# Splitting each weight slot in four passes of 512 columns on GpSimd, and waiting for half a slot on TensorE

## The chip, the cores and the metric

The kernel runs on one core of a Trainium2 chip. The metric is the device time of one execution, in microseconds (us). One profiled execution is read for the prediction; a small number of others were timed without a profile.

## What is computed

Two layers of an encoder trunk over 512 tokens of width 1024, in float32. Each layer is, cut to what matters:

```
h = layer_norm(ALPHA*h + 0.5*swiglu(h, ffn1_wg, ffn1_wu, ffn1_wd))      # 1024 -> 2816 -> 1024
u = h @ w_in                                                            # 1024 -> 8480 columns
y_rw, y_sb, y_hg = rwkv7(u), stick_breaking_attention(u), hgrn2(u)      # three token mixers
mix = (g_rw*(y_rw@w_br_rw) + g_sb*(y_sb@w_br_sb) + g_hg*(y_hg@w_br_hg)) @ w_out
h = layer_norm(ALPHA*h + mix)
h = layer_norm(ALPHA*h + 0.5*swiglu(h, ffn2_wg, ffn2_wu, ffn2_wd))
h = layer_norm(ALPHA*h + sigmoid(h@ple_gate) * (p@ple_proj))
```

Nearly all of the arithmetic is in the dense products with weights that come from HBM.

## The kernel before, in words

**Products.** TensorE works in fp32r, a float32 of fewer mantissa bits. To keep float32 accuracy each operand is split into a high part and a rest: `hT` (the activations, `hT_hi` and `hT_lo`) and the weights (`w_hi` and `w_lo`). A product is three matmuls, high by high, rest by high and high by rest, added up in one PSUM bank (L838, in `products`).

**Slots.** The weights pass through in 468 slots, in a fixed order (`dense_groups`). A slot is 256 rows of a weight matrix, so two blocks `kk` of 128 rows, by up to 512 columns: 128 partitions by 2 by 512 elements. 428 slots have all 512 columns, 32 (the r, k, v projections) have 384, and 8 (the low-rank inputs) have 288. SyncE loads them into `w_raw`, a ring of three (`RAW_RING`). GpSimd splits slot `n` in two passes, each over both blocks at once: L1081 adds a zero and rounds, which gives `w_hi`; L1084 subtracts `w_hi` from the raw weight, which gives `w_lo`. Both go to rings of three slots (`SPLIT_RING`). Between the two passes GpSimd waits on a semaphore of its own (`w_high`), and before a slot it waits for the load and for the release of slot `n-3` by TensorE. SyncE refills a place of `w_raw` after L1084 of its slot.

**TensorE's loop.** `dense` waits for `w_rest_ready` of a slot, which L1084 sets, and then runs for `kk` 0 and 1 over the (mostly four) tiles `m`, three matmuls each: 24 matmuls of 512 columns for a full slot. The release of the slot is set on its last matmul. Where `own_x` is given, block `k` of the activations is waited for as well (`hT_rest`, set by VectorE at L1536; `yT_rest` at L1785; `act_rest`; `mT_rest`). In a group with a `tail`, the last slots are read by all `m` in turn, so that banks finish one after another.

**VectorE.** It has the splits of the activations (L1535 and L1536; L1582 and L1583; L1784 and L1785; L1812 and L1813), the layer norms (L1542 to L1551, then L1570 and L1571, which rescale the residual, eight instructions of 1024 elements), the merge of the branches (L1805 and L1809) and the arithmetic of the mixers (among it L1719 to L1728 of HGRN2, and L578 to L649 of RWKV-7). In the mixers TensorE's order is written by hand: blocks of dense products (`fill`) are put between the mixers' small matmuls.

## Time and profile before

| | us |
|---|---|
| median of 3 runs | 3225.05 |
| lowest and highest | 3222.54 and 3225.9 |
| the profiled execution | 3221.0 |
| its span, first to last instruction | 3219.2 |
| TensorE busy | 3045.5 |
| GpSimd busy | 2104.3 |
| VectorE busy | 1589.3 |

The profiled execution lies 4 us below the median. In the profile PE is TensorE's matmuls, DVE is VectorE, POOL is GpSimd, ACT is ScalarE, and L with a number is a line of the kernel. A duration of POOL or DVE runs from its start to its end, and so includes time in which the instruction was held up after it had started. The ends of matmuls are modelled and reach over the next one's start, so that their pace is read from the distance of the starts.

### The profile page before, as it was taken

The page shows a single profiled execution, that of the slowest core. Times are in us where ns is not written, and L with a number is a line of the kernel's source. Part 1 is how long each engine was busy: PE and PEld are TensorE (multiplying, and loading weights), DVE is VectorE, ACT ScalarE, POOL GpSimd, SP SyncE. Part 2 cuts the span into 40 slices and gives each one's busy share as a digit, 9 for nine tenths or more (in the row PEclk, how much of TensorE's full clock was granted, in tenths as well). Part 3 has the DMA queues.
Part 4 walks back from the last instruction along what each step waited for, and adds up shares of the span by engine and source line. Part 5 has one row for each costly group of instructions (what it writes and reads, how often), then busy time and mean ns, then how long its engine had stood idle before and what let it go on. Part 6 is the DMA issues. An engine that isn't in the chain of part 4 may idle for free. (4 is left out here: it accounts for less than half of the span.)

```text
span 3219.2 us, 45211 instructions
## 1 busy us (share of the span) xinstructions
PE 3045.5 (95%) x19506; PEld 2502.9 (78%) x19506; DVE 1589.3 (49%) x1811; ACT 566.0 (18%) x915; POOL 2104.3 (65%) x941
## 2 busy tenths in 40 slices
PE   8999999889999999999899999998899999999996
PEld 6888787777777878888688887777777778788875
DVE  5321334766656683221882215248666486722127
ACT  1000025443310010000110000353433100100000
POOL 7888675322238878887788877753221578788874
PEclk9999999999999999999899999999999999999998
DMA  4333332111113333323223323311210123333231
GB/s 139 98 96 96 98 118 60 42 49 31 31 40 97 119 97 104 97 94 98 92 92 98 98 93 104 105 55 35 55 40 22 60 88 122 104 99 93 97 105 66
DMA packets 202019, 267.75 MB, mean 83 GB/s; under 512 B 12352, under 2 KB 130460, under 8 KB 201692
## 3 DMA queue, kind: packets, MB, share of 16 engines
q1 hardware_dynamic: 195200, 244.82, 25.1%
q10 hardware_dynamic: 6620, 20.04, 1.8%
q8 instruction: 154, 2.52, 0.3%
q14 instruction: 45, 0.37, 0.0%
HBM read 258.52 MB, written 6.29 MB: 82 GB/s over the span
## 5 line engine op out<-in xcount | busy, mean ns | idle before, releaser
L1081 POOL TENSOR_TENSOR w_hi<-w_raw,zero 128x1024 fp32r<-128x1024 f32 (+2 forms) x468 | 945.7, 2021 | 1040.1 <-PE ps L838 1029.5
L1084 POOL TENSOR_TENSOR w_lo<-w_raw,w_hi 128x1024 fp32r<-128x1024 f32 (+2 forms) x468 | 1160.7, 2480 | 36.8
L838 PE MATMUL ps<-hT_hi,w_hi 128*128 128x512 f32 x2288 | 917.0, 401 | 18.2 <-DVE hT_lo L1536 10.1
L838 PE MATMUL ps<-hT_lo,w_hi 128*128 128x512 f32 x2288 | 897.0, 392 | 0.0
L838 PE MATMUL ps<-hT_hi,w_lo 128*128 128x512 f32 x2288 | 896.7, 392 | 0.0
L838 PEld LDWEIGHTS ps<-hT_hi,w_hi 128*128 128x128 f32 x2288 | 431.7, 189 | 118.5 <-issue 16.5
L838 PEld LDWEIGHTS ps<-hT_hi,w_lo 128*128 128x128 f32 x2288 | 431.8, 189 | 92.7
L838 PEld LDWEIGHTS ps<-hT_lo,w_hi 128*128 128x128 f32 x2288 | 432.5, 189 | 89.0 <-issue 2.9
L1579 DVE TENSOR_TENSOR act_raw<-silu,ps 128x512 f32<-128x512 f32 x88 | 59.8, 680 | 555.7 <-PE ps L838 555.7
L838 PE MATMUL ps<-w_hi,aT_hi 128*128 128x512 f32 x704 | 274.2, 390 | 0.0
L838 PE MATMUL ps<-w_lo,aT_hi 128*128 128x512 f32 x704 | 273.9, 389 | 0.0
L838 PE MATMUL ps<-w_hi,aT_lo 128*128 128x512 f32 x704 | 273.9, 389 | 0.0
L1599 DVE SCALAR_TENSOR_TENSOR h_tok<-ps,h_tok 128x512 f32<-128x512 f32 x48 | 32.7, 681 | 422.5 <-PE ps L838 422.5
L1195 ACT ACTIVATE silu<-ps 128x512 f32<-128x512 f32 x88 | 52.6, 598 | 903.1 <-PE ps L838 899.5
L838 PEld LDWEIGHTS ps<-w_hi,aT_hi 128*128 128x128 f32 x704 | 132.2, 188 | 27.4
L838 PEld LDWEIGHTS ps<-w_hi,aT_lo 128*128 128x128 f32 x704 | 132.2, 188 | 27.4
L838 PEld LDWEIGHTS ps<-w_lo,aT_hi 128*128 128x128 f32 x704 | 132.2, 188 | 27.4
L1583 DVE TENSOR_TENSOR aT_lo<-act_raw,aT_hi 128x512 fp32r<-128x512 f32 x88 | 144.1, 1637 | 3.0
L838 PE MATMUL ps<-w_hi,hT_hi 128*128 128x512 f32 x320 | 129.5, 405 | 4.7 <-DVE hT_lo L1536 4.7
L838 PE MATMUL ps<-w_lo,hT_hi 128*128 128x512 f32 x320 | 126.6, 395 | 0.0
L838 PE MATMUL ps<-w_hi,hT_lo 128*128 128x512 f32 x320 | 126.5, 395 | 0.0
L1582 DVE CAST aT_hi<-act_raw 128x512 fp32r<-128x512 f32 x88 | 109.6, 1246 | 3.0
(297 smaller groups left out, 3667.3 us busy)
## 6 DMA issues: line engine op xcount, KB each, us to landing
w_raw<-in_w_in SPq DMA_DIRECT2D x104, 512.0 KB, 3.6
w_raw<-in_ffn_wg SPq DMA_DIRECT2D x176, 256.0 KB, 2.8
w_raw<-in_ffn_wu SPq DMA_DIRECT2D x176, 256.0 KB, 3.1
w_raw<-in_ffn_wd SPq DMA_DIRECT2D x88, 512.0 KB, 3.6
w_raw<-in_w_in SPq DMA_DIRECT2D x96, 128.0 KB, 2.3
w_raw<-in_w_out SPq DMA_DIRECT2D x16, 512.0 KB, 3.7
w_raw<-in_ple_gate SPq DMA_DIRECT2D x16, 512.0 KB, 3.6
ln_rows<-in_ln_g ACTq DMA_DIRECT2D x8, 512.0 KB, 3.9
```

Source lines behind the costliest of these rows:

```text
L838: ins = nc.tensor.matmul(o, l_, r_, start=first, stop=last)
L1081: nc.gpsimd.tensor_tensor(w_split[0][:, q, :, 0:w], w_raw[:, r, :, 0:w], zero[:, 0:1].unsqueeze(2).to_broadcast([P, 2, w]), ALU.add).then_ ...
L1084: nc.gpsimd.tensor_tensor(w_split[1][:, q, :, 0:w], w_raw[:, r, :, 0:w], w_split[0][:, q, :, 0:w].bitcast(F32), ALU.subtract).then_inc(*st ...
L1195: nc.scalar.activation(silu[:, m, :], b[:, :], ACT.Silu).then_inc(*step("silu_done", L, f, g, m))
L1579: v.tensor_tensor(act_raw[:, m, :], silu[:, m, :], b[:, :], ALU.mult).then_inc(*step("act_raw", L, f, g, m))
L1582: chain(v.tensor_copy(aT[0][:, k, :], act_raw[:, m, :]))
L1583: v.tensor_tensor(aT[1][:, k, :], act_raw[:, m, :], aT[0][:, k, :].bitcast(F32), ALU.subtract).then_inc(*step("act_rest", L, f, k))
L1599: v.scalar_tensor_tensor(z, b[:, :], 0.5 if name == "down" else 1.0, z, ALU.mult, ALU.add).then_inc(*step("res_sum", L, q, half, m))
```

## The change

GpSimd splits a slot in four passes instead of two: for `kk` 0, high part and rest over its columns, then the same for `kk` 1. The semaphores count each half: `w_high` and `w_rest_ready` are set twice for a slot. The wait between high part and rest is kept in each half. TensorE waits for `w_rest_ready` of half `kk` ahead of that half's matmuls; in a tail it waits for the second half, which follows the first on GpSimd. SyncE waits for the second half. Rings, order, loads, the release of slots and all arithmetic are unchanged.

```diff
--- before.py
+++ after.py
@@ -847,8 +847,8 @@
                 at_slot[0] += len(slots)
                 head = len(slots) - tail
                 for i in range(head):
-                    pe.wait_ge(*after("w_rest_ready", n0 + i))
                     for kk in range(2):
+                        pe.wait_ge(*after("w_rest_ready", n0 + i, kk))
                         if own_x is not None:
                             own_x(2 * i + kk)
                         for m in range(n_tiles):
@@ -857,7 +857,7 @@
                 for m in range(n_tiles):
                     for i in range(head, len(slots)):
                         if m == 0:
-                            pe.wait_ge(*after("w_rest_ready", n0 + i))
+                            pe.wait_ge(*after("w_rest_ready", n0 + i, 1))
                         for kk in range(2):
                             if own_x is not None and m == 0:
                                 own_x(2 * i + kk)
@@ -1078,11 +1078,13 @@
                 pool.wait_ge(*after(f"w_in{r}", n))
                 if n >= SPLIT_RING:
                     pool.wait_ge(*after(*slot_free[n - SPLIT_RING]))
-                nc.gpsimd.tensor_tensor(w_split[0][:, q, :, 0:w], w_raw[:, r, :, 0:w],
-                                        zero[:, 0:1].unsqueeze(2).to_broadcast([P, 2, w]), ALU.add).then_inc(*step("w_high", n))
-                pool.wait_ge(*after("w_high", n))
-                nc.gpsimd.tensor_tensor(w_split[1][:, q, :, 0:w], w_raw[:, r, :, 0:w],
-                                        w_split[0][:, q, :, 0:w].bitcast(F32), ALU.subtract).then_inc(*step("w_rest_ready", n))
+                for kk in range(2):
+                    nc.gpsimd.tensor_tensor(w_split[0][:, q, kk, 0:w], w_raw[:, r, kk, 0:w], zero[:, 0:1].to_broadcast([P, w]),
+                                            ALU.add).then_inc(*step("w_high", n, kk))
+                    pool.wait_ge(*after("w_high", n, kk))
+                    nc.gpsimd.tensor_tensor(w_split[1][:, q, kk, 0:w], w_raw[:, r, kk, 0:w],
+                                            w_split[0][:, q, kk, 0:w].bitcast(F32), ALU.subtract).then_inc(
+                        *step("w_rest_ready", n, kk))
 
 
         @block.sync
@@ -1101,7 +1103,7 @@
                     pieces, g, i = slot_list[n]
                     r = n % RAW_RING
                     if n >= RAW_RING:
-                        sp.wait_ge(*after("w_rest_ready", n - RAW_RING))
+                        sp.wait_ge(*after("w_rest_ready", n - RAW_RING, 1))
                     if g[0][0] == "rkv" and g[0][2] == 1 and i == 3:
                         load_rwkv(g[0][1])
                     for src, at, w in pieces:
```

## Rows read from the trace of the kernel before

**Rows 1.** The page, part 1: engine, busy us, share of span, instructions.

```profile
PE 3045.5 (95%) x19506; PEld 2502.9 (78%) x19506; DVE 1589.3 (49%) x1811; ACT 566.0 (18%) x915; POOL 2104.3 (65%) x941
```

**Rows 2.** Waits of TensorE: waiter, awaited, us in total, times, longest.

```profile
PE ps L894 <- DVE h_tok L1551: 29.6, 15, 4.2
...
PE ps L838 <- DVE hT_lo L1536: 14.8, 7, 2.3
...
PE ps L838 <- POOL w_lo L1084: 4.0, 1, 4.0
```

**Rows 3.** Timeline of GpSimd: start us, duration us, what, idle time before.

```profile
55.13 1.89 POOL L1081 TENSOR_TENSOR w_hi<-w_raw,zero 128x1024 fp32r<-128x1024 f32 x1 [1.01 <-PE ps L838]
...
57.10 2.38 POOL L1084 TENSOR_TENSOR w_lo<-w_raw,w_hi 128x1024 fp32r<-128x1024 f32 x1
...
564.67 1.15 POOL L1081 TENSOR_TENSOR w_hi<-w_raw,zero 128x576 fp32r<-128x576 f32 x1 [1.00 <-PE ps L838]
...
565.89 1.40 POOL L1084 TENSOR_TENSOR w_lo<-w_raw,w_hi 128x576 fp32r<-128x576 f32 x1
```

**Rows 4.** Timeline of TensorE where one slot ends, another begins.

```profile
409.10 0.39 PE L838 MATMUL ps<-hT_hi,w_lo 128*128 128x512 f32 x1
...
409.33 0.39 PE L838 MATMUL ps<-hT_hi,w_hi 128*128 128x512 f32 x1
```

**Rows 5.** Windows: us, busy us of each engine, granted clock; last column GB/s.

```profile
109.53:131.29 21.76, 21.76 (x98) 18.02 (x97) 6.58 (x6) 1.20 (x2) 18.18 (x8) 1.00 0.32 97
...
16.00:20.00 4.00, 4.00 (x11) 3.13 (x11) 3.96 (x3) 0.00 (x0) 3.92 (x2) 0.57 0.41 131
```

**Rows 6.** Timeline of the start, three engines.

```profile
13.36 2.40 POOL L1084 TENSOR_TENSOR w_lo<-w_raw,w_hi 128x1024 fp32r<-128x1024 f32 x1
...
13.60 2.71 DVE L1536 TENSOR_TENSOR hT_lo<-h_raw,hT_hi 128x512 fp32r<-128x512 f32 x1
...
15.81 0.50 PE L838 MATMUL ps<-hT_hi,w_hi 128*128 128x512 f32 x1 [3.99 <-POOL w_lo L1084]
...
18.38 2.75 DVE L1536 TENSOR_TENSOR hT_lo<-h_raw,hT_hi 128x512 fp32r<-128x512 f32 x1
...
35.64 0.50 PE L838 MATMUL ps<-hT_hi,w_hi 128*128 128x512 f32 x1 [1.75 <-DVE hT_lo L1536]
```

**Rows 7.** Timeline, VectorE, without a GpSimd pass beside it.

```profile
36.57 0.42 DVE L1535 CAST hT_hi<-h_raw 128x512 fp32r<-128x512 f32 x1
...
37.02 0.69 DVE L1536 TENSOR_TENSOR hT_lo<-h_raw,hT_hi 128x512 fp32r<-128x512 f32 x1
```

**Rows 8.** Timelines after a norm, GpSimd's passes and TensorE's first use.

```profile
404.23 2.87 POOL L1081 TENSOR_TENSOR w_hi<-w_raw,zero 128x1024 fp32r<-128x1024 f32 x1
...
419.52 3.26 POOL L1084 TENSOR_TENSOR w_lo<-w_raw,w_hi 128x1024 fp32r<-128x1024 f32 x1
...
425.65 0.39 PE L838 MATMUL ps<-hT_hi,w_hi 128*128 128x512 f32 x1
```

**Rows 9.** Timelines of the first layer norm, VectorE and GpSimd.

```profile
384.89 2.48 DVE L1551 TENSOR_SCALAR h_tok<-h_tok,ln_mv,ln_rstd 128x1024 f32<-128x1024 f32 x1
...
384.94 1.89 POOL L1081 TENSOR_TENSOR w_hi<-w_raw,zero 128x1024 fp32r<-128x1024 f32 x1
```

**Rows 10.** Timelines of the merge, VectorE and TensorE.

```profile
1037.91 2.73 DVE L1785 TENSOR_TENSOR yT_lo<-y_raw,yT_hi 128x512 fp32r<-128x512 f32 x1
...
1035.94 0.47 PE L838 MATMUL ps<-yT_hi,w_hi 128*128 128x512 f32 x1 [0.76 <-issue]
...
1040.70 0.50 PE L838 MATMUL ps<-yT_hi,w_hi 128*128 128x512 f32 x1 [1.77 <-DVE yT_lo L1785]
```

**Rows 11.** Groups by line and shape: count, busy us, mean ns, idle us before.

```profile
L1721 DVE TENSOR_TENSOR hg_p<-hg_p 128x1024 f32<-128x1024 f32 x14 | 25.7, 1837 | 0.5
```

**Rows 12.** Timeline of VectorE in the HGRN2 part, one free instruction.

```profile
617.30 1.22 DVE L1721 TENSOR_TENSOR hg_p<-hg_p 128x1024 f32<-128x1024 f32 x1
```

**Rows 13.** Windows: the mixer of one layer.

```profile
560.00:935.00 375.00, 334.30 (x4524) 274.61 (x4523) 243.49 (x392) 140.20 (x222) 104.85 (x56) 0.96 0.13 36
```

## The prediction

> **What bounds the kernel now.** I read the page's busy line first, then the waits, then the timelines of single stretches. TensorE is busy for 95% of the span, GpSimd for 65% [rows 1]. So only some 174 us in which TensorE does nothing can be won, and the question is whom it waits for then. The waits say: mostly VectorE. Its layer norms hold TensorE for 29.6 us and the split of the activations for 14.8 us; GpSimd's split of the weights holds it once, for 4.0 us, at the start [rows 2]. That the change lets TensorE begin on half a slot is therefore worth little in itself. What can matter is that GpSimd and VectorE hold each other up, and that the change alters the size of the pieces.
>
> **How close GpSimd is to being the bound.** Where nothing disturbs it, a full slot costs GpSimd 1.89 us for the high part and 2.38 us for the rest [rows 3], 4.36 us with the gaps. TensorE starts a matmul every 0.227 us, with no gap where one slot ends and the next begins although a wait stands there [rows 4], so it takes 24 x 0.227 = 5.44 us for a slot. GpSimd has 1.08 us to spare for each slot. In a stretch of four slots of the first FFN layer with VectorE at work beside it, it was busy for 18.18 of 21.76 us [rows 5].
>
> **Part 1: the added passes.** A pass of half the size costs more than half. The passes over 1024 and 576 elements took 1.89 and 1.15 us (high part), 2.38 and 1.40 us (rest) [rows 3]: 1.65 and 2.19 ns for an element, so 0.20 and 0.14 us that don't shrink. A pass over 512 elements then takes 1.04 and 1.26 us. A slot becomes 2 x (1.04 + 1.26) + 2 x 0.08 (the wait between high part and rest) = 4.76 us, 0.40 us more than now; for the line's other end, a fixed part of nothing, it is 0.08 us more. Beside TensorE's 5.44 us both are hidden: in the FFN stretch 18.18 us of passes, 0.32 us of gaps and 4 x 0.40 give 20.1 of 21.76 us [rows 5]. Value taken: 0.40 us a slot on GpSimd, nothing on the path. If the cover is gone, each further 0.1 us on each of the 176 slots of the FFN's first products costs 18 us.
>
> **Part 2: the added waits.** TensorE gets a second wait in each slot. Queued behind it are that half's 12 matmuls. The half has long been ready, and a satisfied wait at a slot's boundary showed no gap [rows 4]: nothing. SyncE's wait, with the refill queued behind it, ends 0.40 us later, and that place of the three-deep ring is read only after two more slots: nothing. GpSimd's added wait is in the 4.76 us.
>
> **Part 3: the start.** TensorE's first product begins at 15.81 us, when the first slot is whole [rows 6]. With half a slot it begins 1.89 + 2.38 - 1.04 - 1.26 = 1.97 us earlier, at 13.84. Then TensorE needs a new block of activations every 12 x 0.227 = 2.72 us, but VectorE gives one only every 4.78 us (13.60 to 18.38 [rows 6]). Its two instructions need 0.42 and 0.69 us when alone [rows 7]; they are held up by GpSimd's passes: the one issued at 13.60 ends 0.55 us after the w_lo pass of 13.36 [rows 6]. So the pace is one pair of passes and 0.5 us. With half passes it is 1.04 + 1.26 + 0.5 and some 0.05 more, 2.85 us, and since TensorE starts with a block in hand, it no longer waits noticeably. The sixth block begins at 35.64 us now [rows 6]. It would begin at 13.84 + 5 x 2.72 + 1.5 = 28.9, where 1.5 us is what the half clock costs: in 4 us at a granted clock of 0.57 [rows 5] 11 matmuls ran in place of 17.6. Gain 6.7 us. Bounds: 2.0 us (the half slot alone, VectorE's pace unchanged) and 8.2 us (the shorter pause also spares the low clock).
>
> **Part 4: the merge.** At the end of the first half of the merge TensorE waits 0.76 and 1.77 us for the split of the next branch [rows 10]. VectorE has been busy without a break before that; one such instruction took 2.73 us in place of 0.69 [rows 7, 10]. In this stretch four tiles follow one another with three instructions each that a pass can hold up. Held up by half passes, each loses at most 1.0 to 1.3 us in place of 1.5 to 2.0, though more of them are hit; I take 0.5 us of gain for each of the last three tiles and 1 us for each block of the split, 3.5 us, which is more than the 2.5 us of waiting. Gain 2.5 us in each layer, 5.0 in all; bounds 0 and 5.0.
>
> **Part 5: the layer norms.** There are seven with TensorE waiting. In the first, VectorE's L1551 was issued at 384.89 us, waited through the pass of 384.94 to 386.83 and ended 0.54 us after it [rows 9]; alone it would need about 0.8 us. With half passes I laid the same instructions out. L1551 of the tile before is held up too, so this one is issued near 385.35, during a rest pass that ends near 385.7. If VectorE is let in then, it ends near 386.2 and TensorE's next product starts 0.9 us earlier than now. If GpSimd's queued high part goes first, as here, L1551 ends near 387.2, and the two instructions of the split behind it meet one pass each where one of them met none: 0.4 us later than now. Value: nothing; bounds over seven norms -6 and +3 us.
>
> The Trainium skill ("SBUF — State Buffer", Who interferes with whom) says that VectorE and GpSimd share one port pair, that an instruction holds it for its whole length, and that issue order decides who is blocked. This row speaks against the last of these: VectorE was issued 0.05 us ahead of the pass and still came after it. By the page's rule the norms would gain the 6 us; rival B is that case.
>
> **Part 6: the mixers.** Here VectorE often sets the end, and TensorE is idle for 41 of 375 us in a layer [rows 13]. The 14 instructions of L1721 took 1.84 us on the mean [rows 11] against 1.22 us when free [rows 12]: 0.6 us lost by each. An instruction that comes alone loses less to a half pass. In a dense chain, where each of VectorE's instructions meets a pass, what is lost is the whole time of the passes, and that grows from 4.27 to 4.60 us a slot. With some 25 slots in each layer's mixers, a third of that growth on VectorE and half of it on the path, this is 50 x 0.33 / 6 = 2.8 us lost; lone instructions give back 0.8. Value: +2 us; bounds -9 (0.6 us on some 45 instructions are 27 us of delay in a layer; halved, and a third of it felt, that is 4.5) and +20 us (0.4 us on each of 50 slots, all of it felt).
>
> **Part 7: the stretches where GpSimd falls behind.** After a norm L1570 and L1571, eight long instructions, alternate with the passes: the passes take 2.87 and 3.26 us, and a slot 6.2 us, more than TensorE's 5.44. The slot done at 422.78 us is first used at 425.65: 2.87 us ahead [rows 8]. Four such slots cost 3.0 us of the lead, which was 5.9. With four passes in a slot each meets one such instruction, which adds (2.87 - 1.89 + 3.26 - 2.38) / 2 = 0.93 us: a slot takes 4.76 + 3.7 = 8.5 us, but only two slots instead of four, since the eight instructions are used up sooner. That costs 6.1 us of the lead. But the pass that ends last is needed only 2.72 us after the slot's first product: 5.9 - 6.1 + 2.7 = 2.5 us stay. Nothing; if that cover is gone, 1 to 2 us in each of six places.
>
> **The sum.** -6.7 - 5.0 + 0 + 2.0 = -9.7 us. It is made against the profiled execution (span 3219.2 us, time 3221.0). The median of the runs lies 4 us above that, and I set the change against the median: 3225.05 - 9.7 = 3215.3 us.
>
> **The rivals.**
> A, forecast, 3215 us (its own range 3209 to 3221), chance 0.46.
> B, VectorE is let in at each end of a pass, so that none of its instructions loses more than one short pass: norms -6, mixers -9. 3225 - 6.7 - 5 - 6 - 9 = 3198 us. For it: at the start VectorE does come in after both kinds of pass [rows 6]. Against: the norm [rows 9]. Chance 0.17.
> C, only the start gains and the mixers take it back: -6.7 + 5 = 3223 us, no difference that can be measured. For it: one of the merge's two waits is put down to no one [rows 10], so the split needn't be what is late, and the bounds of parts 3, 4 and 6 allow it. Against: the two gains are on the path, TensorE stands still there [rows 6, 10]. Chance 0.21.
> D, slower: the dense chains. More passes stand in VectorE's way in the mixers, each taking its turn. Price up to 0.6 us a slot on 50 slots, 30 us, against 11.7 us gained: 3243 us. It decides from (11.7 + 6.5) / 50 = 0.36 us a slot. For it: VectorE is the late one there [rows 11, 12]. Against: the ports' added time is only 0.33 us a slot. Chance 0.11.
> E, slower too: GpSimd becomes the bound. If a pass has 0.15 us more of fixed time than the line gives, an FFN slot is 0.2 us over 5.44: 176 x 0.2 = 35 us, 3248 us. Chance 0.05.
>
> 0.2% (6.5 us) is about what a measurement of this kernel can tell from no change. Faster by more: B and five sixths of A (below 3218.6), 0.55. Within: C and the rest of A, 0.29. Slower: D, E, 0.16. The range leaves out D and E, 0.16, and takes in B and the slow side of C: 3196 to 3233 us.
>
> **What would show it.** TensorE's first product near 13.8 us and the sixth block near 29; passes of 1.04 and 1.26 us; the waits at the merge gone; L1551 in the norms still held up, by less; GpSimd near 20 of 21.76 us in an FFN stretch with TensorE's pace still 0.227 us; no wait of TensorE for w_lo after the start. A pass above 1.2 or 1.4 us, or VectorE's mixer instructions longer on the mean than now, would prove it wrong.

## The result, and the profile after

The changed kernel takes 3192.1 us (median of 4 runs, 3191.0 to 3193.9) against 3225.0 us for the kernel before on the same chip: a ratio of 0.990 (95% interval 0.988 to 0.992). It is 33 us faster, not 10, and lies 4 us below the range. The profiled execution took 3191.0 us with a span of 3189.2 us, so the traces differ by 30.0 us, and that is the amount that has to be found. Line numbers from L1081 on differ by one or two: L1081 and L1084 are now L1082 and L1085, L1535 and L1536 are L1537 and L1538, L1551 is L1553, L1721 is L1723, L1785 is L1787.

The page's busy line after:

```profile
PE 3035.5 (95%) x19506; PEld 2497.7 (78%) x19506; DVE 1401.0 (44%) x1811; ACT 566.3 (18%) x915; POOL 2316.1 (73%) x1877
```

Against [rows 1], TensorE runs the same 19506 matmuls in 10.0 us less busy time: summed over its trace the granted clock was at its lower level (1.2 GHz) for 129.8 us, before for 156.7. The other 20.0 us are pauses. VectorE, with the same 1811 instructions, is busy for 188 us less, and nothing of its own work was changed. GpSimd has twice the passes and 212 us more. So VectorE's instructions had been held up, and are held up less.

The waits of TensorE after (waiter, awaited, us in total, times, longest):

```profile
PE ps L894 <- DVE h_tok L1553: 23.8, 16, 3.8
PE ps L838 <- DVE hT_lo L1538: 19.0, 7, 3.2
...
PE ps L838 <- POOL w_lo L1085: 3.5, 2, 1.8
...
PE ps L539 <- DVE rhs L738: 1.7, 8, 0.2
...
PE ps L479 <- DVE invT L723: 1.1, 2, 0.6
```

Against [rows 2] the norms gave up 5.8 us and the split of the activations took 4.2 of them back. L539, RWKV-7's small matmuls inside the mixer, had 6.6 us in 14 waits before, the longest 1.4, and L479 had 5.0 us. Those two, which my prediction never looked at, gave back 8.8 us; L371 took 2.8 back (9.3 us in 6 waits, before 6.5 in 5).

By stage, from the starts of TensorE's matmuls at the stages' borders in the two traces, the 30.0 us are: the start 5.5; the mixers 7.9 and 5.8 (layer 0 and 1); the merge 3.7 and 5.2; the product with the embeddings and its norm (between the layers) 2.4; one FFN with its norm 1.1; some 1.5 us are lost again in small pieces. Each of these figures is the difference of one execution and one other. In parts of the mixers where nothing was changed such a difference reached 7.0 us (table at the last experiment), so the split by stages is rough, and what it says of single layers rougher still.

GpSimd's passes where nothing disturbs them (timeline of GpSimd: start us, duration us, what):

```profile
70.71 1.04 POOL L1082 TENSOR_TENSOR w_hi<-w_raw,zero 128x512 fp32r<-128x512 f32 x1
71.83 1.29 POOL L1085 TENSOR_TENSOR w_lo<-w_raw,w_hi 128x512 fp32r<-128x512 f32 x1
73.07 1.04 POOL L1082 TENSOR_TENSOR w_hi<-w_raw,zero 128x512 fp32r<-128x512 f32 x1
74.19 1.28 POOL L1085 TENSOR_TENSOR w_lo<-w_raw,w_hi 128x512 fp32r<-128x512 f32 x1
75.43 1.04 POOL L1082 TENSOR_TENSOR w_hi<-w_raw,zero 128x512 fp32r<-128x512 f32 x1
```

A slot takes 75.43 - 70.71 = 4.72 us there; 4.76 was worked out. Windows of the start and of an FFN stretch as in [rows 5] (same columns):

```profile
16.00:20.00 4.00, 4.00 (x18) 2.89 (x17) 3.96 (x4) 0.00 (x0) 3.92 (x4) 1.00 0.41 131
102.00:123.76 21.76, 21.76 (x98) 18.02 (x97) 6.02 (x6) 1.20 (x3) 20.86 (x18) 1.00 0.37 115
```

GpSimd is busy for 20.86 of 21.76 us in the second, where 18.18 stood before, and TensorE's pace is the same. In the first the granted clock is 1.00 where it was 0.57: 18 matmuls in 4 us, not 11.

The start, as in [rows 6], over all engines:

```profile
12.49 1.63 DVE L1538 TENSOR_TENSOR hT_lo<-h_raw,hT_hi 128x512 fp32r<-128x512 f32 x1
...
13.63 0.50 PE L838 MATMUL ps<-hT_hi,w_hi 128*128 128x512 f32 x1 [1.79 <-POOL w_lo L1085]
...
15.34 1.67 DVE L1538 TENSOR_TENSOR hT_lo<-h_raw,hT_hi 128x512 fp32r<-128x512 f32 x1
...
31.32 3.13 DVE L1643 TENSOR_SCALAR h_tok<-h_tok 128x4096 f32<-128x4096 f32 x1
...
32.37 3.19 POOL L1085 TENSOR_TENSOR w_lo<-w_raw,w_hi 128x512 fp32r<-128x512 f32 x1
...
35.62 0.50 PE L838 MATMUL ps<-hT_hi,w_hi 128*128 128x512 f32 x1 [1.70 <-POOL w_lo L1085]
```

The first product begins at 13.63 us and VectorE gives a block every 2.85 us, as worked out. The sixth block begins at 28.02 us, before at 35.64. Two things were missed. Beside VectorE's splits a pair of passes takes as long as VectorE's pair, a slot 5.76 us (passes at 13.54 and 19.30), more than TensorE's 5.44, so that GpSimd's lead shrinks. And then comes one long instruction of VectorE, L1643 over 4096 elements: the pass that starts at 32.37 takes 3.19 us instead of 1.29, and TensorE waits 1.70 us for its `w_lo` at 35.62. Before, the same instruction (L1641) came later, at 37.63.

**Where the mixers' gain sits.** RWKV-7 hands small results from TensorE to VectorE (L738) and back (L539), with one block of dense matmuls between. VectorE puts one long instruction of its own between two L738. Before (all engines, timeline):

```profile
812.54 2.14 DVE L626 TENSOR_TENSOR rw_dec<-k_inv,rw_e 128x512 f32<-128x512 f32 x1
...
814.74 2.71 DVE L630 SCALAR_TENSOR_TENSOR rw_kk<-rw_kk,rw_ss 128x512 f32<-128x512 f32 x1
...
814.87 0.27 PE L539 MATMUL ps<-rhs,pq 64*64 64x64 f32 x2 [0.23 <-DVE rhs L738]
...
817.37 0.21 DVE L738 TENSOR_TENSOR rhs<-ps,rhs 128x64 f32<-128x64 f32 x1
...
817.64 0.27 PE L539 MATMUL ps<-rhs,pq 64*64 64x64 f32 x2 [1.44 <-DVE rhs L738]
```

And after, the same instructions:

```profile
800.89 1.28 DVE L626 TENSOR_TENSOR rw_dec<-k_inv,rw_e 128x512 f32<-128x512 f32 x1
...
802.23 1.64 DVE L630 SCALAR_TENSOR_TENSOR rw_kk<-rw_kk,rw_ss 128x512 f32<-128x512 f32 x1
...
803.79 0.21 DVE L738 TENSOR_TENSOR rhs<-ps,rhs 128x64 f32<-128x64 f32 x1
...
804.18 0.27 PE L539 MATMUL ps<-rhs,pq 64*64 64x64 f32 x2
```

L630 is held up in both. An exchange with its dense block takes TensorE some 1.27 us (L539 at 812.02, next at 813.30). Before, L626 takes 2.14 us instead of 0.68 and TensorE stands still for 0.23 us; then L630 takes 2.71 instead of 0.68, and it stands still for 1.44 us. After, they take 1.28 and 1.64 us, and the dense work covers both: the row of L539 shows no idle time of TensorE ahead of it. So in this row of exchanges hold-ups of up to 1 us cost nothing, one of 1.5 us costs 0.2, and one of 2 us right behind it 1.4.

### The profile page after: what moved, and what is told of

Its sections match the earlier page's. It is cut to its first block and busy times, and to the rows that moved or that the text cites. A ratio compares the mean times of both kernels' runs of the same rounds, so it can differ in the third digit from the quotient of the medians.

```text
span 3189.2 us, 46255 instructions
## 1 busy us (share of the span) xinstructions
PE 3035.5 (95%) x19506; PEld 2497.7 (78%) x19506; DVE 1401.0 (44%) x1811; ACT 566.3 (18%) x915; POOL 2316.1 (73%) x1877
## 5 line engine op out<-in xcount | busy, mean ns | idle before, releaser
L1082 POOL TENSOR_TENSOR w_hi<-w_raw,zero 128x512 fp32r<-128x512 f32 (+2 forms) x936 | 1058.8, 1131 | 764.7 <-PE ps L838 754.6
L1085 POOL TENSOR_TENSOR w_lo<-w_raw,w_hi 128x512 fp32r<-128x512 f32 (+2 forms) x936 | 1283.3, 1371 | 73.5
L838 PE MATMUL ps<-hT_hi,w_hi 128*128 128x512 f32 x2288 | 916.0, 400 | 18.7 <-DVE hT_lo L1538 12.6
L838 PE MATMUL ps<-hT_hi,w_lo 128*128 128x512 f32 x2288 | 895.6, 391 | 0.0
L838 PE MATMUL ps<-hT_lo,w_hi 128*128 128x512 f32 x2288 | 895.6, 391 | 0.0
L838 PEld LDWEIGHTS ps<-hT_hi,w_hi 128*128 128x128 f32 x2288 | 431.0, 188 | 119.0 <-POOL w_lo L1085 15.6
L838 PEld LDWEIGHTS ps<-hT_hi,w_lo 128*128 128x128 f32 x2288 | 430.9, 188 | 92.9
L838 PEld LDWEIGHTS ps<-hT_lo,w_hi 128*128 128x128 f32 x2288 | 431.6, 189 | 88.2 <-issue 2.9
L838 PE MATMUL ps<-w_hi,aT_hi 128*128 128x512 f32 x704 | 274.3, 390 | 0.0
L838 PE MATMUL ps<-w_lo,aT_hi 128*128 128x512 f32 x704 | 274.0, 389 | 0.0
L838 PE MATMUL ps<-w_hi,aT_lo 128*128 128x512 f32 x704 | 273.9, 389 | 0.0
L838 PEld LDWEIGHTS ps<-w_hi,aT_lo 128*128 128x128 f32 x704 | 132.2, 188 | 27.5
L838 PEld LDWEIGHTS ps<-w_hi,aT_hi 128*128 128x128 f32 x704 | 132.2, 188 | 27.4
L838 PEld LDWEIGHTS ps<-w_lo,aT_hi 128*128 128x128 f32 x704 | 132.2, 188 | 27.2
L838 PE MATMUL ps<-w_hi,hT_hi 128*128 128x512 f32 x320 | 129.2, 404 | 6.4 <-DVE hT_lo L1538 6.4
L1585 DVE TENSOR_TENSOR aT_lo<-act_raw,aT_hi 128x512 fp32r<-128x512 f32 x88 | 126.6, 1439 | 3.0
L838 PE MATMUL ps<-w_hi,hT_lo 128*128 128x512 f32 x320 | 126.5, 395 | 0.0
L838 PE MATMUL ps<-w_lo,hT_hi 128*128 128x512 f32 x320 | 126.4, 395 | 0.0
L1179 ACT ACTIVATE ln_rstd<-ln_mv,ln_eps 128x1 f32<-128x1 f32 x32 | 9.4, 295 | 498.7 <-DVE ln_mv L1550 498.7
```

Source lines behind the costliest of these rows:

```text
L838: ins = nc.tensor.matmul(o, l_, r_, start=first, stop=last)
L1082: nc.gpsimd.tensor_tensor(w_split[0][:, q, kk, 0:w], w_raw[:, r, kk, 0:w], zero[:, 0:1].to_broadcast([P, w]), ALU.add).then_inc(*step("w_h ...
L1085: nc.gpsimd.tensor_tensor(w_split[1][:, q, kk, 0:w], w_raw[:, r, kk, 0:w], w_split[0][:, q, kk, 0:w].bitcast(F32), ALU.subtract).then_inc( ...
L1179: nc.scalar.activation(ln_rstd[:, t, :], ln_mv[:, t, 1:2], ACT.Sqrt, bias=ln_eps[:, :]).then_inc(*step("ln_sqrt", L, q, t))
L1585: v.tensor_tensor(aT[1][:, k, :], act_raw[:, m, :], aT[0][:, k, :].bitcast(F32), ALU.subtract).then_inc(*step("act_rest", L, f, k))
```

## The experiments

Two theories stood at the beginning. **H**: the time comes from VectorE being held up by shorter passes. **W**: it comes from TensorE's waits on half a slot. All kernels below have the following frame in place of the changed kernel's loop, with `split_parts` giving the passes of a slot as (first block, block after the last, first column, column after the last). Frame and changed kernel do the same where `split_parts` gives `[(0, 1, 0, w), (1, 2, 0, w)]`, a high and a rest pass over each half, four passes in all. The lines added at the top shift all numbers: L838 of before is L849 to L853 here, L1084 is L1097 to L1103. The kernel before was timed again beside each group of kernels, with medians from 3221.1 to 3224.4 us; where two kernels of different groups are compared, I give the difference of their gains too where it is another.

```diff
+        def last_part(n, kk):
+            return max(j for j, p in enumerate(parts_of(n)) if p[0] <= kk < p[1])
...
-                        pe.wait_ge(*after("w_rest_ready", n0 + i, kk))
+                        pe.wait_ge(*after("w_rest_ready", n0 + i, last_part(n0 + i, kk)))
...
-                for kk in range(2):
+                for j, (k0, k1, c0, c1) in enumerate(parts_of(n)):
```

### TensorE waits for the whole slot

```diff
 def split_parts(name, n, w):
     return [(0, 1, 0, w), (1, 2, 0, w)]
...
+                    pe.wait_ge(*after("w_rest_ready", n0 + i, last_part(n0 + i, 1)))
                     for kk in range(2):
-                        pe.wait_ge(*after("w_rest_ready", n0 + i, kk))
```

> Four passes for each slot as in the changed kernel, but TensorE waits for the whole slot at its top, as before the change. Theory H (short passes hold VectorE up for less): nearly all of the 33 us stay, and only the start loses 1 to 3 us, so 3193 to 3196 us. Rival W (what pays is that TensorE may begin on half a slot): most of the gain goes, 3215 us or more.

Measured: 3204.6 us, ratio 0.994 (0.992 to 0.996). Both theories missed; it lies between them. Its wait of TensorE for GpSimd:

```profile
PE ps L849 <- POOL w_lo L1099: 10.7, 10, 4.4
```

These are 10.7 us in ten waits, 7.2 more than after. By stages the mixers gain 7.1 and 4.7 us and the merge 3.7 and 5.2, where the changed kernel gains 7.9 and 5.8, 3.7 and 5.2: there the waits are worth little. Most of the 13.9 us between the two traces is lost at the start (3.0 us), in the first FFN of layer 1 (3.2), in the embeddings' stage (1.9) and at the end (2.2), places where GpSimd has fallen behind. So of the 33 us 18 to 20 need only the shorter passes, and 13 to 15 us need the half waits, as long as the FFNs have four passes (12.5 us between the medians of the two kernels, 13.9 between the traces, 15 between the gains).

### Four passes in the mixers and the merge alone

```diff
 def split_parts(name, n, w):
+    return [(0, 1, 0, w), (1, 2, 0, w)] if name[0] in ("sb", "hg", "lora", "rkv", "gate", "branch", "out") else [(0, 2, 0, w)]
```

> Four passes only for the slots of the mixers, the merge and the output projection (sb, hg, lora, rkv, gate, branch, out); two passes for all others. Between the two traces the mixers and the merge had shed 21.5 us of the 30. Theory H: 3225 - 21 = 3204 us, within 3 us. If the places interact (a shorter hold-up in one stage is given back in another) it is 3209 us or more.

Measured: 3193.4 us, ratio 0.991 (0.989 to 0.992), as fast as the whole change, and better than I expected. By stages: mixers 6.7 and 7.7 us, merge 3.7 and 5.2, the output product with its norm 1.4 in each layer, where the changed kernel loses 0.5. The FFNs' four passes and the start's gain come out even.

### Four passes everywhere else

```diff
 def split_parts(name, n, w):
+    return [(0, 2, 0, w)] if name[0] in ("sb", "hg", "lora", "rkv", "gate", "branch", "out") else [(0, 1, 0, w), (1, 2, 0, w)]
```

> The complement: four passes for the slots of the FFNs and of the per-layer gate, two in the mixers and the merge. The traces had 5.5 us at the start and 2.9 us around the norms: 3225 - 8.4 = 3217 us, within 3 us. Below 3210 us would say that the mixers' gain is not made by the passes that run in the mixers.

Measured: 3218.7 us, ratio 0.9985 (0.9976 to 0.9995). The start gains 5.3 us in its trace; in the norms and FFNs hardly anything moves but the embeddings' stage (2.4). So this is the part of the change that I had priced rightly, and the other is the one that I had priced wrongly.

### Eight passes in the mixers

If hold-ups by the length of a pass are the cause, halving again must gain again. The eight-pass slots are those of HGRN2's level computation, the low-rank inputs, the r, k, v projections and the first group of gate and branch.

```diff
 def split_parts(name, n, w):
+    if name[0] in ("hg", "lora", "rkv") or name in [(b, L, 0, 0) for b in ("gate", "branch") for L in range(DEPTH)]:
+        return [(k, k + 1, c, c + w // 2) for k in range(2) for c in (0, w // 2)]
     return [(0, 1, 0, w), (1, 2, 0, w)]
```

> As the changed kernel, but eight passes of at most 256 columns for the slots of hg, lora, rkv and the first gate and branch, where GpSimd has much idle time. Theory H: each hold-up halves again while each pass costs 0.2 or 0.14 us more of fixed time, so another 4 to 7 us in the mixers: 3185 to 3188 us. The rule of my prediction (a chain loses the whole time of the passes, which grows by some 0.7 us a slot): 3195 to 3202 us.

Measured: 3172.1 us, ratio 0.984 (0.983 to 0.986), 20 us below the changed kernel (17 by the gains) and better than expected. The mixers gain 18.0 and 16.7 us against before.

### Nearly no split in the mixers

The same slots, but only 16 of their columns are split, with the same count of passes as in the changed kernel. The split of the other columns is left out, so the products of these slots use what the rings hold.

```diff
     if name[0] in ("hg", "lora", "rkv") or name in [(b, L, 0, 0) for b in ("gate", "branch") for L in range(DEPTH)]:
+        return [(0, 1, 0, 16), (1, 2, 0, 16)]
```

> As the changed kernel, but for the slots of hg, lora, rkv and the first gate and branch GpSimd splits only 16 of the columns, so that VectorE is held up there hardly at all; the other columns' split is left out. It measures what all hold-ups in this stretch cost. Theory H: more than the 50 us below before that eight passes reached; of VectorE's delay in the stretch under eight passes about a half is felt, so 3155 to 3168 us. If eight passes had gained by something else than shorter hold-ups, this run would be no faster than 3172 us.

Measured: 3150.8 us, ratio 0.978 (0.976 to 0.979). This is what the mixers cost when GpSimd is out of VectorE's way: another 21 us below eight passes. Loads, waits and matmuls are all there, and TensorE waits for `w_lo` as long as with eight passes (3.0 us against 2.8), so these 21 us are not a late GpSimd.

The windows of that stretch in the four kernels, each between the same two matmuls, both layers (us, then busy us of PE, PEld, DVE, ACT and POOL, granted clock, DMA share, GB/s). Before:

```profile
582.23:930.80 348.57, 312.09 (x4429) 257.75 (x4428) 234.46 (x378) 121.95 (x201) 92.58 (x48) 0.96 0.13 35
2176.74:2521.90 345.16, 308.45 (x4429) 254.94 (x4428) 235.66 (x378) 121.82 (x201) 93.06 (x48) 0.97 0.13 36
```

After:

```profile
576.22:916.87 340.65, 309.48 (x4429) 256.12 (x4428) 231.03 (x378) 121.99 (x201) 114.31 (x96) 0.96 0.13 36
2156.52:2497.32 340.80, 309.57 (x4430) 256.06 (x4428) 230.71 (x378) 121.95 (x201) 115.47 (x96) 0.96 0.13 36
```

Eight passes:

```profile
577.60:908.22 330.62, 306.68 (x4430) 254.42 (x4428) 218.03 (x378) 122.22 (x201) 152.36 (x192) 0.98 0.13 37
```

Nearly no split:

```profile
577.24:896.99 319.75, 302.92 (x4429) 251.50 (x4428) 201.76 (x378) 121.97 (x201) 35.99 (x96) 0.99 0.14 39
```

The more passes, the longer GpSimd is busy (92.6, 114.3, 152.4 us in a layer) and the shorter is the stretch (348.6, 340.7, 330.6). Worked out from the rows of VectorE in both layers (the hold-up is an instruction's duration less the shortest of the same line and shape in these five traces; a hit is one of over 0.15 us; the times at the low clock are the spells of the lower granted clock). The column with sixteen passes is of a later experiment:

| passes in a slot | two | four | eight | sixteen | nearly none |
|---|---|---|---|---|---|
| length of the stretch, us | 693.7 | 681.5 | 660.6 | 667.1 | 641.4 |
| hold-up of VectorE, us | 82 | 74 | 46 | 27 | 14 |
| hits | 72 | 114 | 122 | 62 | 16 |
| mean of a hit, us | 1.05 | 0.58 | 0.30 | 0.24 | 0.36 |
| longest hit, us | 2.06 | 0.96 | 0.45 | 0.38 | 0.39 |
| TensorE idle, us | 73.2 | 62.4 | 47.5 | 54.3 | 33.8 |
| TensorE at the low clock, us | 54.6 | 47.8 | 27.3 | 30.7 | 17.1 |

### High, high, rest, rest

In the changed kernel a rest pass starts 0.08 us after the end of its high part, since GpSimd waits for its own semaphore; that pause could be what lets VectorE in. Here the order of a slot's passes is changed, and the pause is gone.

```diff
-                for kk in range(2):
-                    nc.gpsimd.tensor_tensor(w_split[0][...], w_raw[...], zero[...], ALU.add).then_inc(*step("w_high", n, kk))
-                    pool.wait_ge(*after("w_high", n, kk))
-                    nc.gpsimd.tensor_tensor(w_split[1][...], ..., ALU.subtract).then_inc(*step("w_rest_ready", n, kk))
+                for j, (k0, k1, c0, c1) in enumerate(parts_of(n)):
+                    nc.gpsimd.tensor_tensor(w_split[0][...], w_raw[...], zero[...], ALU.add).then_inc(*step("w_high", n, j))
+                for j, (k0, k1, c0, c1) in enumerate(parts_of(n)):
+                    pool.wait_ge(*after("w_high", n, j))
+                    nc.gpsimd.tensor_tensor(w_split[1][...], ..., ALU.subtract).then_inc(*step("w_rest_ready", n, j))
```

> Four passes of the same sizes as in the changed kernel, in the order high, high, rest, rest instead of high, rest, high, rest. The half slot is complete 1.04 us later; the idle moment of 0.08 us between a high part and its rest, in which VectorE can get in, is gone. If VectorE gets in at the end of any pass, as theory H in its plain form says, the time is that of the changed kernel within 3 us (3189 to 3196 us at 3222 of before). If it gets in mainly at those idle moments, hold-ups join to longer ones and 10 us or more of the gain go: 3200 us or more.

Measured: 3188.9 us, ratio 0.989 (0.988 to 0.991), no slower than the changed kernel. Timelines of VectorE and GpSimd (x2 is two passes in a row):

```profile
61.20 16.45 DVE L1596 CAST aT_hi<-act_raw 128x512 fp32r<-128x512 f32 x1
...
70.34 2.54 POOL L1097 TENSOR_TENSOR w_lo<-w_raw,w_hi 128x512 fp32r<-128x512 f32 x2
72.84 2.04 POOL L1093 TENSOR_TENSOR w_hi<-w_raw,zero 128x512 fp32r<-128x512 f32 x2
74.83 2.53 POOL L1097 TENSOR_TENSOR w_lo<-w_raw,w_hi 128x512 fp32r<-128x512 f32 x2
77.51 2.48 POOL L1093 TENSOR_TENSOR w_hi<-w_raw,zero 128x512 fp32r<-128x512 f32 x2
...
1196.38 21.58 DVE L1596 CAST aT_hi<-act_raw 128x512 fp32r<-128x512 f32 x1
...
1575.96 9.44 DVE L1842 TENSOR_TENSOR h_tok<-h_tok,ple_pr 128x512 f32<-128x512 f32 x1
```

The time is as theory H in its plain form has it, but the trace isn't. The passes of 61.37 to 77.36 us stand without a gap, and all that time one instruction of VectorE, 0.43 us long when alone, doesn't come in: it ends at 77.65, after the first pause of GpSimd (0.15 us, from 77.36 to 77.51). The other two rows are the same: the one ends at 1217.96, where GpSimd paused from 1217.69 on, the other 0.55 us after GpSimd's last pass in a row. All three are the second instruction after VectorE had been idle for 13 to 16 us. The next longest hold-up in this trace is 1.12 us, so most of its some 500 hits were over by the end of one pass; and no kernel that waits between high part and rest has an instruction of VectorE of over 4 us. So the end of a pass is mostly enough for VectorE to come in, but not always. The last of the three stands ahead of a norm, for which TensorE waits 8.6 us; the longest such wait of the other kernels is 4.4. Of the four executions (3184.0, 3185.2, 3192.5 and 3193.2 us) the profiled one took the longest; whether the shorter ones have such hold-ups isn't known, nor what decides whether VectorE comes in at the end of a pass.

### A mix of the three

Eight passes where they gain, four in the other slots of mixers and merge and in the first eight slots of all, two in the FFNs.

```diff
 def split_parts(name, n, w):
     if name[0] in ("hg", "lora", "rkv") or name in [(b, L, 0, 0) for b in ("gate", "branch") for L in range(DEPTH)]:
         return [(k, k + 1, c, c + w // 2) for k in range(2) for c in (0, w // 2)]
+    if name[0] in ("sb", "hg", "lora", "rkv", "gate", "branch", "out") or n < 8:
+        return [(0, 1, 0, w), (1, 2, 0, w)]
+    return [(0, 2, 0, w)]
```

> Eight passes for hg, lora, rkv and the first gate and branch, four for the other mixer slots, the merge, the output projection and the first eight slots of the program, two for all other FFN slots. With two passes there the norms and what follows them took some 3 us less in each layer than with four (second run against the changed kernel). Sum of the stages: 3172 - 6 = 3166 us; 3172 us if these stages interact with the mixers.

Measured: 3167.7 us, ratio 0.983 (0.981 to 0.985). It beats both kernels, the changed one by 24 us (22 by the gains). Its busy line and its wait for GpSimd:

```profile
PE 3028.6 (96%) x19506; PEld 2493.3 (79%) x19506; DVE 1471.7 (47%) x1811; ACT 566.9 (18%) x915; POOL 2326.6 (74%) x1661
```

```profile
PE ps L853 <- POOL w_lo L1103: 2.9, 2, 1.7
```

VectorE is busy for 71 us more than in the changed kernel, since in the FFNs it meets long passes again, and the kernel is faster all the same: TensorE's waits for VectorE at the norms and at the split of the activations are 39.9 us in all, 42.8 in the changed kernel.

### The half waits where the FFNs have two passes

The kernel with four passes in mixers and merge alone, with the wait for the whole slot of the first experiment.

```diff
+                    pe.wait_ge(*after("w_rest_ready", n0 + i, last_part(n0 + i, 1)))
                     for kk in range(2):
-                        pe.wait_ge(*after("w_rest_ready", n0 + i, kk))
```

> As the run with four passes in the mixers only, but TensorE waits for the whole slot everywhere. Theory: the half waits are only a cover for GpSimd being late, which it is in the FFN stages when they have four passes; where those have two, the half waits are worth nothing, and this gives 3193 us like its twin, within 3 us. If the half waits gain by themselves, it is 3198 us or more.

Measured: 3195.6 us, ratio 0.991 (0.990 to 0.993); its twin with half waits took 3193.4. The intervals overlap. The half waits are worth 13 to 15 us with four passes in the FFNs and 2 us, or nothing, with two. So they don't gain by themselves; they cover what the four passes cost in the FFNs.

### Sixteen passes in the mixers

As the mix, with passes of a quarter of the columns in that stretch.

```diff
     if name[0] in ("hg", "lora", "rkv") or name in [(b, L, 0, 0) for b in ("gate", "branch") for L in range(DEPTH)]:
+        return [(k, k + 1, c * (w // 4), (c + 1) * (w // 4)) for k in range(2) for c in range(4)]
```

> As the seventh run (3167.7 us), but sixteen passes of at most 128 columns in place of eight for hg, lora, rkv and the first gate and branch. Under two, four and eight passes VectorE's delay in the two stretches of the RWKV part and the HGRN2 levels was 82, 74 and 46 us and the stretches took 694, 681 and 661 us; with almost no split they took 641 us. Theory H: the hold-ups halve again to 0.15 us on the mean, a delay near 25 us, 8 to 14 us gained: 3154 to 3160 us. A full slot would then cost GpSimd 7.1 us, beyond TensorE's 5.44; if GpSimd becomes the late one in these stretches, 3168 us or more.

Measured: 3176.9 us, ratio 0.985 (0.984 to 0.987), 9 us more than the mix (11 by the gains). TensorE's wait for GpSimd:

```profile
PE ps L853 <- POOL w_lo L1103: 9.8, 6, 2.4
```

VectorE's hold-up falls to 27 us as theory H has it, but a pass of 96 to 128 columns still costs 0.43 to 0.55 us on the mean, and now TensorE waits for GpSimd, 9.8 us instead of 2.9. Where the end of splitting lies depends on the place. The part with HGRN2's levels is 15 us longer than in the mix (206.2 us against 191.1 in both layers), the part with RWKV-7's exchanges 6 us shorter (272.5 against 278.4; both parts as in the table at the last experiment). Sixteen passes in the second part alone weren't tried.

### Eight passes everywhere

```diff
 def split_parts(name, n, w):
+    return [(k, k + 1, c, c + w // 2) for k in range(2) for c in (0, w // 2)]
```

> Eight passes of 256 columns for every slot. In the mixers it is the run of 3172 us. In the FFNs a slot costs GpSimd 5.55 us alone and some 0.4 us more with VectorE's instructions beside it, against TensorE's 5.44: GpSimd is the bound there, 0.1 to 0.5 us on each of some 350 slots, and later in the merge. 3172 + 60 to 170 us: 3230 to 3340 us. If the fixed part of a pass cost nothing where VectorE is held up, it would stay below 3200 us.

Measured: 3331.9 us, ratio 1.034 (1.032 to 1.036). A slot of eight passes (0.61 and 0.73 us each) takes 5.55 us by itself, against TensorE's 5.44. TensorE's wait for GpSimd, and a window of the first FFN:

```profile
PE ps L849 <- POOL w_lo L1099: 95.5, 141, 4.5
```

```profile
100.00:121.76 21.76, 21.23 (x92) 16.21 (x91) 4.74 (x6) 1.20 (x2) 20.59 (x31) 1.00 0.27 83
```

It starts 92 matmuls where the changed kernel starts 98 in as long a time. Each of the four stretches of an FFN is 24 to 26 us longer than before. This is rival E, one size of pass further on.

### Four and eight passes in the first gate group alone

These eight slots (four in each layer) lie beside RWKV-7's exchanges shown above.

```diff
 def split_parts(name, n, w):
+    return [(0, 1, 0, w), (1, 2, 0, w)] if name in [("gate", L, 0, 0) for L in range(DEPTH)] else [(0, 2, 0, w)]
```

> The kernel before with four passes in only 8 of its 468 slots, those of the first gate group of each layer, whose splits run while TensorE and VectorE exchange small results in the RWKV part. Theory S (at each exchange TensorE has some 1.3 us of other work: a hold-up of up to 1 us is covered by it, one of 1.5 to 2 us is not): these 8 slots alone bring 5 to 9 us, 3213 to 3217 us at 3222 of before. If a hold-up cost its share wherever it falls, 8 slots of the 116 that gave 22 us would bring 1.5 us, which can't be told from no change.

```diff
 def split_parts(name, n, w):
+    return [(k, k + 1, c, c + w // 2) for k in range(2) for c in (0, w // 2)] if name in [("gate", L, 0, 0) for L in range(DEPTH)] else [(0, 2, 0, w)]
```

> The same with eight passes in these 8 slots. Theory S: what four passes leave of the hold-ups is mostly covered already, so that the second halving adds less than the first, 1 to 3 us (3211 to 3215 us). If the time followed the sum of the delays, it would add as much again, 5 us or more.

Measured: 3215.8 us, ratio 0.997 (0.996 to 0.998), with four, and 3218.1 us, ratio 0.998 (0.997 to 0.999), with eight, at 3224.4 of before. By the medians four passes in 8 of 468 slots gain 8.6 us, more than a quarter of the whole change, and eight gain 6.3; the two intervals overlap, and the nine times of the first reach from 3209.0 to 3221.7 us. So the medians show that these slots count, but not which of the two is better. The traces show it, part by part (both layers, between the same matmuls in all kernels: HGRN2's levels are matmul 2464 to 2997 and 12217 to 12750, RWKV-7's exchanges 4500 to 6892 and 14253 to 16645; worked out from the rows of TensorE and the granted clock):

| | before | two passes in mixers | four in 8 slots | eight in 8 slots | the change | eight in mixers | sixteen in mixers |
|---|---|---|---|---|---|---|---|
| HGRN2's levels, us | 208.6 | 210.8 | 215.6 | 213.8 | 203.2 | 192.1 | 206.2 |
| TensorE idle in them, us | 33.4 | 33.1 | 33.7 | 33.2 | 28.5 | 21.3 | 32.4 |
| at the low clock in them, us | 30.8 | 34.2 | 47.8 | 44.4 | 27.4 | 13.6 | 23.9 |
| RWKV-7's exchanges, us | 288.0 | 288.7 | 280.5 | 278.4 | 281.1 | 278.4 | 272.5 |

The 8 slots make the whole gain in the exchanges: 7.5 us with four passes, where the whole change has 6.9, and 9.6 us with eight, as many as with eight passes in the mixers. So the second halving does add some 2 us there, 1 us in each layer, less than the first, as theory S has it, and sixteen passes add 6 us more. A hold-up under 1 us costs little in that place, but not nothing. What eight passes gain beyond that in the mixers, 11.1 us at HGRN2's levels and 7.2 between the two parts (190.0 us against 197.2 with the change), lies in the other slots.

The first four columns have the same passes at HGRN2's levels, and the same idle time of TensorE within 0.6 us, yet they take 208.6 to 215.6 us there: the low clock lasted for 30.8 to 47.8 us. The trace of before is the shortest of the four, so that the gain of the change in that part, 5.4 us against it, would be 8 to 12 us against the other three.

## Why the prediction was right and wrong

**Part 1, the passes: right.** 1.04 and 1.29 us against 1.04 and 1.26, a slot 4.72 us against 4.76, 20.86 us in the FFN stretch against 20.1. TensorE's pace there didn't change.

**Part 2, the added waits, and part 7: right, but the cover was priced too low.** That no time is lost on a satisfied wait holds. Part 7 counted on the second half being needed only 2.72 us later, and in the changed kernel this cover held: after its first product TensorE waits for `w_lo` once, for 1.70 us. Without it I had 1 to 2 us in each of six places; the first experiment has 13 to 15 us, 3.0 of them at the start, so that the change is worth 18 us and not 33.

**Part 3, the start: right, the size a little off.** -5.5 us against -6.7. Up to the sixth block it is -7.6 us, for the clock did better than I took it (the upper bound of 8.2 us was for this). Behind it 2 us go again: a GpSimd slot of 5.76 us beside VectorE's splits was forgotten, since I used 4.76 us, the undisturbed one, for GpSimd and the disturbed one for VectorE, and so was L1643, which lengthens one pass by 1.9 us.

**Part 4, the merge: right in place, too small.** -8.9 us against -5.0. Both waits of [rows 10] are gone. The timeline of VectorE in the merge of the changed kernel:

```profile
1013.55 1.66 DVE L1815 TENSOR_TENSOR mT_lo<-m_acc,mT_hi 128x512 fp32r<-128x512 f32 x1
1015.13 1.26 DVE L1786 CAST yT_hi<-y_raw 128x512 fp32r<-128x512 f32 x1
1016.42 1.66 DVE L1787 TENSOR_TENSOR yT_lo<-y_raw,yT_hi 128x512 fp32r<-128x512 f32 x1
```

Where one instruction took 2.73 us none takes over 1.67, and each pair needs 2.88 us. My bound of 5.0 us was the sum of the waits that I saw, and they are what went: behind the first branch TensorE is idle for 2.5 and 2.6 us in the two merges before and for nothing after. The rest is in the time that it is busy, where the low clock has a part: in layer 1 the merge had a spell of 3.4 us of it before and none after. These spells vary. In the traces of kernels that left the merge alone it took 174.4 to 176.0 us in layer 0 and 185.0 to 186.7 in layer 1; in the changed kernel it took 171.2 and 181.9.

**Part 5, the norms: right.** Nothing was forecast; -0.2 to +0.6 us came out in five of the seven stages with a norm, -1.1 in one and -2.4 in the embeddings' one. In the first norm, before (VectorE, behind the row of [rows 9]):

```profile
388.62 1.25 DVE L1535 CAST hT_hi<-h_raw 128x512 fp32r<-128x512 f32 x1 [1.24 <-ACT h_raw L1168]
389.91 0.69 DVE L1536 TENSOR_TENSOR hT_lo<-h_raw,hT_hi 128x512 fp32r<-128x512 f32 x1
```

And in the changed kernel, GpSimd, VectorE and TensorE:

```profile
379.98 1.04 POOL L1082 TENSOR_TENSOR w_hi<-w_raw,zero 128x512 fp32r<-128x512 f32 x1
...
379.91 1.66 DVE L1553 TENSOR_SCALAR h_tok<-h_tok,ln_mv,ln_rstd 128x1024 f32<-128x1024 f32 x1
382.81 1.17 DVE L1537 CAST hT_hi<-h_raw 128x512 fp32r<-128x512 f32 x1 [1.24 <-ACT h_raw L1170]
384.02 1.63 DVE L1538 TENSOR_TENSOR hT_lo<-h_raw,hT_hi 128x512 fp32r<-128x512 f32 x1
```

```profile
385.75 0.77 PE L838 MATMUL ps<-hT_hi,w_hi 128*128 128x512 f32 x1 [3.03 <-DVE hT_lo L1538]
386.32 0.63 PE L838 MATMUL ps<-hT_lo,w_hi 128*128 128x512 f32 x1
386.75 0.63 PE L838 MATMUL ps<-hT_hi,w_lo 128*128 128x512 f32 x1
```

As laid out by hand: L1553 takes 1.66 us instead of the 2.48 of [rows 9], but of the two instructions of the split behind it both now meet a pass, and before only the first did: 1.17 and 1.63 us against 1.25 and 0.69. What L1553 gains, 0.82 us, the second of them gives back, 0.94. Behind the pause the starts of TensorE's matmuls are 0.43 us apart, and not 0.227.

**Part 6, the mixers: wrong in sign and size.** +2 us was the value, -13.7 us came out, below the bound of -9. This step and not the others makes the error: 15.7 of the 20.3 us between the two sums (3.9 are the merge). The figure of 13.7 us is itself good to some us only, as the last experiment shows; the sign isn't in doubt, for four passes in mixers and merge alone gain 29 us by the medians. Three things in it failed.
- *Each of VectorE's instructions meets a pass, so what is lost is the whole time of the passes.* In the stretch of the table the hold-up is 82 us where GpSimd is busy for 186, and 74 where it is busy for 230. With eight passes it is 46 of 306. The number of hits rose from 72 to 114, not to 144, and their mean fell from 1.05 to 0.58 us, by more. In the whole trace it fell from 561 to 372 us, with 382 and 523 hits of 1.44 and 0.69 us on the mean.
- *A third of the delay is felt.* What is felt isn't a share. In the exchanges above it is what of a hold-up goes beyond the other work that TensorE has there. Halving the longest hits (2.06 to 0.96 us) therefore takes more than the next halving does: 7.5 and then 2.1 us in the last experiment. The row of L1721 [rows 11], on which I rested this part, fell from a mean of 1837 to 1591 ns only, and said nothing of RWKV-7's exchanges, where 6.9 of the stretch's 12.2 us were.
- *A us less of waiting is a us less of time.* The clock adds to it: the time at the low clock fell from 156.7 to 129.8 us, and TensorE's busy time by 10.0 us with it. I had priced the clock at the start alone.

The Trainium skill ("SBUF — State Buffer", Who interferes with whom) says that VectorE and GpSimd hold their shared port pair for the length of an instruction and that issue order decides. The first half agrees with the table as an upper bound, where GpSimd pauses between high part and rest: the longest hit is 2.06, 0.96 and 0.45 us beside rest passes of 2.38, 1.29 and 0.73 us. The second half doesn't agree here either, by the starts that the profile gives: L1553 is issued at 379.91 us, 0.07 ahead of the pass of 379.98, and ends 0.55 us behind it; and the instruction issued at 61.20 in the kernel without pauses comes after all the passes that started from 61.37 to 77.36.

**The rivals.** B was nearest in its time (3198 us) and in the mixers' sign, but not in its reason: it had the norms gain 6 us, and they gained next to nothing. C and D had the mixers lose by more passes; up to eight passes in a slot the tables show the opposite. E is true, but one size of pass further on.

## What to carry to other kernels

Where two engines hold each other up, the length of a single instruction on the one mostly sets how long a handover of the other can slip, as long as the one pauses now and then, and what counts is that slip less the other work of the waiting engine, handover by handover, not the sum of the delays. Split the helper's work finely where the held-up engine is on the path, coarsely where the helper itself is near the pace (here eight passes, 5.55 us of GpSimd for a slot alone and more beside VectorE, against 5.44 us of TensorE, made 110 us), and price a removed pause with what the clock gives back behind it: here 10 us for 20 us of pauses. Read what a stage gains from more than one trace of the kernel before: the low clock's spells alone moved one part by 7 us.

## What was not expected of the hardware

A stream of passes without pauses can shut an instruction of VectorE out for 9 to 22 us, and a pause of 0.15 us was enough to let it in. The longest hold-up stays 0.3 us short of a rest pass in the stretch of the table, at all three sizes, and in the whole trace 0.2 us (2.20 and 1.10 us with two and four passes); why, no run here shows. Two instructions of VectorE and GpSimd that alternate settle into one rhythm, 1.26 and 1.66 us on VectorE against 0.42 and 0.69 alone, and 1.35 to 1.6 us on GpSimd against 1.04 and 1.29 alone.

Two things stay open. The stage of the embeddings' product and its norm is 2.4 us shorter in the changed kernel, and as much in the kernels with four passes only in the mixers and only outside of them, but 0.4 to 0.5 us in those of the first and fourth experiment. Around it (matmul 9500 to 10300) TensorE is idle for 1.5 us less than before and at the low clock for 3.4 us less (17.1 us against 20.5), and the low clock differs among the others too; what sets it there, no run shows. And the first gate group's eight slots gain 8.6 us with four passes by the medians, while the one trace of that kernel is as long as that of before (3219.9 us against 3219.2): it gains 7.5 us in the exchanges and loses 7.0 at HGRN2's levels, where nothing was changed.
